# Stick-breaking attention: suffix sums in two float32r passes, mask by TensorE, both heads' exponentials together

## The reference

```python
z = jnp.einsum('bqhd,bkhd->bhqk', qb, kk).astype(jnp.float32) * scale
mask = (k_pos[None, :] < q_pos[:, None])[None, None]
log_beta = jax.nn.log_sigmoid(z)
log_one_minus = jnp.where(mask, jax.nn.log_sigmoid(-z), 0.0)
suffix = lax.cumsum(log_one_minus, axis=3, reverse=True) - log_one_minus
A = jnp.where(mask, jnp.exp(log_beta + suffix), 0.0)
outs.append(jnp.einsum('bhqk,bkhd->bqhd', A.astype(v.dtype), vv))
```

## Time and profile before

| | us |
|---|---|
| median of 3 runs | 4930.05 |
| lowest, highest | 4927.13, 4930.28 |
| the profiled execution | 4933.49 |
| its span, first to last instruction | 4931.4 |
| TensorE busy | 4438.4 (90%) |
| VectorE busy | 2837.3 (58%) |
| ScalarE busy | 1843.0 (37%) |
| mean granted TensorE clock | 0.958 |

### The profile page before, as it was taken

One profiled execution on the slowest core, in us unless ns is written; L12 is line 12 of the kernel. 1 busy time (PEld: TensorE's weight loads), 2 busy tenths in 40 slices (PEclk: granted clock), 3 DMA queues, 4 the chain that ended last, 5 costly groups with the idle time before them and its releaser, 6 DMA issues. The chain is left out here.

```text
span 4931.4 us, 59891 instructions
## 1 busy us (share of the span) xinstructions
PE 4438.4 (90%) x22171; PEld 3698.0 (75%) x22171; DVE 2837.3 (58%) x5051; ACT 1843.0 (37%) x2602; POOL 413.9 (8%) x308
## 2 busy tenths in 40 slices
PE   7988888878998466999999996999999999899998
PEld 5867775645874256999999995766878877677887
DVE  0777776683436897888888885334343333444332
ACT  1655644443321033333333333346232233643322
POOL 0000000000002601232222320000000000000000
PEclk9999999999999798999999998999999999999999
DMA  7111111102221036777777771211323322122232
GB/s 261 56 39 39 35 35 43 39 13 90 90 77 61 10 137 229 280 269 281 271 277 280 270 278 63 72 48 45 101 90 98 95 75 66 37 73 92 95 96 84
DMA packets 195952, 578.14 MB, mean 117 GB/s; under 512 B 17328, under 2 KB 66736, under 8 KB 194352
## 3 DMA queue, kind: packets, MB, share of 16 engines
q1 hardware_dynamic: 157888, 433.77, 25.9%
q0 software_dynamic: 36864, 134.23, 8.0%
q10 hardware_dynamic: 1008, 7.55, 0.4%
HBM read 548.22 MB, written 27.26 MB: 117 GB/s over the span
## 5 line engine op out<-in xcount | busy, mean ns | idle before, releaser
L402 DVE TENSOR_TENSOR tile_rest<-tile_raw,tile_up 128x1024 fp32r<-128x1024 f32 (+2 forms) x288 | 338.6, 1180 | 781.9 <-ACT tile_up L393 781.6
L410 PE MATMUL layer_psum<-hn_up,tile_up 128*128 128x512 f32 x1344 | 535.0, 398 | 21.2 <-DVE hn_rest L497 21.2
L411 PE MATMUL layer_psum<-hn_up,tile_rest 128*128 128x512 f32 x1344 | 527.3, 392 | 0.0
L412 PE MATMUL layer_psum<-hn_rest,tile_up 128*128 128x512 f32 x1344 | 527.0, 392 | 0.0
L393 ACT ACTIVATE tile_up<-tile_raw 128x1024 fp32r<-128x1024 f32 (+2 forms) x288 | 291.4, 1018 | 369.1 <-PE layer_psum L412 368.5
L2186 PE MATMUL ex_psum<-ex_t_up,ex_u_up 128*128 128x384 f32 x1024 | 344.5, 336 | 10.5 <-ACT ex_prod L2260 6.2
L2204 PE MATMUL ex_psum<-ex_prod_up,ex_v_up 128*128 128x384 f32 x1024 | 342.9, 335 | 3.9 <-DVE xT L2326 3.9
L2187 PE MATMUL ex_psum<-ex_t_up,ex_u_rest 128*128 128x384 f32 x1024 | 344.0, 336 | 0.0
L2188 PE MATMUL ex_psum<-ex_t_rest,ex_u_up 128*128 128x384 f32 x1024 | 343.9, 336 | 0.0
L2206 PE MATMUL ex_psum<-ex_prod_rest,ex_v_up 128*128 128x384 f32 x1024 | 342.6, 335 | 0.0
L2205 PE MATMUL ex_psum<-ex_prod_up,ex_v_rest 128*128 128x384 f32 x1024 | 342.6, 335 | 0.0
(11 more groups left out here) (440 smaller groups left out, 10140.1 us busy)
## 6 DMA issues: line engine op xcount, KB each, us to landing
ex_u<-in_peer_u SPq DMA_DIRECT2D x128, 512.0 KB, 6.8
tT<-in_peer_v SPq DMA_DIRECT2D x128, 512.0 KB, 7.4
tile_raw<-in_w_gu SPq DMA_DIRECT2D x88, 512.0 KB, 3.5
xT<-in_w_head SPq DMA_DIRECT2D x56, 512.0 KB, 3.5
mod_w<-in_w_ada SPq DMA_DIRECT2D x48, 512.0 KB, 4.8
mg_w_raw<-in_w_merge SPq DMA_DIRECT2D x48, 512.0 KB, 3.5
expert_table<-et_rows SPq DMA_DIRECT2D x6, 4096.0 KB, 13.3
ex_rows<-expert_table SPq DMA_DIRECT2D x64, 384.0 KB, 8.0
```

Of the source, the lines that this page charges most:

```text
L402: self.nc.vector.tensor_tensor(out=self.rest[:, n % self.SLOTS, 0:blocks, :], in0=self.raw[n % self.RAWS][:, 0:blocks, :], in1=self.up[:, ...
L410: self.nc.tensor.matmul(dst, w_up, up, start=first, stop=False)
L411: self.nc.tensor.matmul(dst, w_rest, up, start=False, stop=False)
L412: return self.nc.tensor.matmul(dst, w_up, rest, start=False, stop=last)
```

## The change

The scores' accumulation group gets one more float32r matmul per key block, which adds -2^30 at and below the diagonal of the block's first 128 columns. That takes the place of all eight multiplies by the mask. The scores go to SBUF in one VectorE copy of 1280 columns a head; ScalarE takes |z| straight from PSUM. The term that is summed becomes max(z, 0) + ln(1 + exp(-|z|)), in one VectorE instruction. ScalarE rounds it to float32r (`up`), VectorE takes the remainder (`low`), and the sums are twenty float32r matmuls a head with negative constants. The triangle includes the key itself, so z plus the sums is the power. ScalarE's order becomes |z|, exp, |z|, exp, ln, ln, and both projections stand ahead of both sums on TensorE. Three float32r constants are made by ScalarE at the start of layer 0's stage, and the first scores wait for them. `z` lies in the tables' memory, so layer 1's retention loads the tables again, and VectorE waits for that. Cut to its core:

```diff
-    AT = [0, 512, 896, 1152]
+    AT = [0, 512, 1024, 896]
@@ stage_retention
     def sync(sp):
         if first:
             w.load_to(sp, base + 2)
-            sp.dma_start(mem.tab[:], io["tables"]).then_inc(tables, 16)
+        else:
+            for powered in earlier.powered:
+                sp.wait_ge(powered, START + 12)
+        sp.dma_start(mem.tab[:], io["tables"]).then_inc(tables, 16)
         w.load_to(sp, sk + 10)
@@ vector
-            dve.wait_ge(tables, START + 16)
+        dve.wait_ge(tables, START + 16)
         for n in range(4):
             w.cut_rest(dve, q_of(0) + n + 4)
@@ stage_sticks, tensor
+            if layer == 0 and i == 0 and hh == 0:
+                pe.wait_ge(signs, START + 3)
             for c in ORDER:
-                nc.tensor.matmul(part(hh, c), k[rows, c * P:(c + 1) * P], q[rows, c * P:T],
-                                 start=True, stop=True).then_inc(scored[hh], 1)
+                nc.tensor.matmul(part(hh, c), k[rows, c * P:(c + 1) * P], q[rows, c * P:T], start=True, stop=False)
+                ins = nc.tensor.matmul(part(hh, c)[:, 0:P], mem.minus["far"][:], mem.minus["later"][:],
+                                       start=False, stop=True)
+            ins.then_inc(scored[hh], 1)
@@
-            pe.wait_ge(rested[hh], START + 3 * i + 3)
+            pe.wait_ge(low_ready[hh], START + i + 1)
...
+                    for piece in (up[hh], low[hh]):
+                        ins = nc.tensor.matmul(dst[:, (c2 - c) * P:T - c * P], sign, piece[:, AT[c2]:AT[c2] + n],
@@
             project(0, Q_AT[i + 1] if following else mx)
+            project(1, Q_AT[i + 1] + 1 if following else mx + 1)
             sums(i, 0)
-            project(1, Q_AT[i + 1] + 1 if following else mx + 1)
             sums(i, 1)
             output(i, 0)
@@ scalar
+        def exponentials(i, hh):
+            act.wait_ge(scored[hh], START + i + 1)
...
+            if i > 0 and hh == 0:
+                act.wait_ge(sb_cut, START + i)
+            nc.scalar.activation(beta[hh][:], every(hh), ACT.Abs).then_inc(soft[hh], 1)
+            act.wait_ge(soft[hh], START + i * 4 + 1)
+            nc.scalar.activation(beta[hh][:], beta[hh][:], ACT.Exp, scale=-1.0).then_inc(soft[hh], 1)
...
+        def halves(i, hh):
+            act.wait_ge(raised[hh], START + i + 1)
+            nc.scalar.activation(up[hh][:], beta[hh][:], ACT.Copy).then_inc(up_ready[hh], 1)
...
+        if layer == 0:
+            nc.scalar.activation(mem.minus["later"][:], mem.c("later"), ACT.Copy, scale=-1.0).then_inc(signs, 1)
+            nc.scalar.activation(mem.minus["ones"][:], mem.c("ones"), ACT.Copy, scale=-1.0).then_inc(signs, 1)
+            nc.scalar.activation(mem.minus["far"][:], mem.c("ident"), ACT.Copy, scale=-FAR).then_inc(signs, 1)
         for i in range(PAIRS):
+            exponentials(i, 0)
+            exponentials(i, 1)
             logs(i, 0)
             logs(i, 1)
...
+            between(i, 0)
+            halves(i, 0)
+            halves(i, 1)
+            tile(i, 0)
+            between(i, 1)
+            tile(i, 1)
+            weights(i, 0)
+            weights(i, 1)
@@ vector
         for i in range(PAIRS):
...
+            copies(i, 0)
+            copies(i, 1)
+            raises(i, 0)
+            raises(i, 1)
+            halves(i, 0)
+            halves(i, 1)
+            tile(i, 0)
+            powers(i, 0)
+            tile(i, 1)
+            powers(i, 1)
@@ constants
-           "later": (r[:, None] > r[None, :]) * 1.0,
-           "before": (r[:, None] < r[None, :]) * 1.0,
+           "later": (r[:, None] >= r[None, :]) * 1.0,
```

More of the change, by code:

```diff
@@ L42 @@
 CONSTS = [("ones", P), ("mean_d", P), ("mean_head", P), ("mean_ret", P), ("ident", P), ("swap", P),
-          ("later", P), ("before", P), ("iota", P), ("eps", 1), ("one", 1),
+          ("later", P), ("iota", P), ("eps", 1), ("one", 1),
           ("cos2", T), ("sin2", T)]
@@ L2403, with stage_retention @@
 Retention = namedtuple("Retention", "sync tensor scalar vector sk_out rstd_ready cut")
-Sticks = namedtuple("Sticks", "sync tensor scalar vector o_out sig_done cut")
+Sticks = namedtuple("Sticks", "sync tensor scalar vector o_out sig_done cut powered")
 Stage = namedtuple("Stage", "sync tensor scalar vector norm")
-def stage_retention(nc, io, mem, ph, local, layer, norm=None):
+def stage_retention(nc, io, mem, ph, local, layer, norm, earlier):
     F = 6
@@ L2745, in sums @@
                     n = T - c2 * P
-                    ins = nc.tensor.matmul(dst[:, (c2 - c) * P:T - c * P],
-                                           mem.c("later") if c2 == c else mem.c("ones"),
-                                           rest[hh][:, AT[c2]:AT[c2] + n], start=c2 == c, stop=c2 == TB - 1)
-                ins.then_inc(summed[hh], 1)
+                    sign = mem.minus["later"][:] if c2 == c else mem.minus["ones"][:]
+                    for piece in (up[hh], low[hh]):
+                        ins = nc.tensor.matmul(dst[:, (c2 - c) * P:T - c * P], sign, piece[:, AT[c2]:AT[c2] + n],
+                                               start=c2 == c and piece is up[hh],
+                                               stop=c2 == TB - 1 and piece is low[hh])
+                if c != 1:
+                    ins.then_inc(summed[hh], 1)
         def output(i, hh):
@@ L2856, in scalar @@
                 act.wait_ge(o_out[hh], START + i + 1)
-            nc.scalar.activation(mem.sb_up[:, i, :], o[:], ACT.Copy).then_inc(sb_up_ready, 1)
+            nc.scalar.activation(mem.sb_up[:, i, :], o, ACT.Copy).then_inc(sb_up_ready, 1)
         w.cut_up(act, mx + 6)
     def vector(dve):
-        def before(hh, data):
-            for c in range(TB):
-                ins = nc.vector.tensor_tensor(out=data[:, AT[c]:AT[c] + P], in0=data[:, AT[c]:AT[c] + P],
-                                              in1=mem.c("before"), op=ALU.mult)
-            return ins
@@ new lines, in raises, with halves @@
+        def raises(i, hh):
+            dve.wait_ge(soft[hh], START + i * 4 + 3)
+            dve.wait_ge(copied[hh], START + i + 1)
+            nc.vector.scalar_tensor_tensor(out=beta[hh][:], in0=z[hh], scalar=0.0, in1=beta[hh][:], op0=ALU.max,
+                                           op1=ALU.add).then_inc(raised[hh], 1)
+        def halves(i, hh):
+            dve.wait_ge(up_ready[hh], START + i + 1)
+            nc.vector.tensor_tensor(out=low[hh][:], in0=beta[hh][:], in1=up[hh][:].bitcast(F32),
+                                    op=ALU.subtract).then_inc(low_ready[hh], 1)
@@ L2879, in powers @@
         def powers(i, hh):
-            for c, made in zip(ORDER, MADE):
-                dve.wait_ge(summed[hh], START + i * TB + made)
-                cols = slice(AT[c], AT[c] + T - c * P)
-                nc.vector.tensor_tensor(out=beta[hh][:, cols], in0=beta[hh][:, cols], in1=part(hh, c),
+            for bank in range(3):
+                dve.wait_ge(summed[hh], START + i * 3 + bank + 1)
+                cols = slice(bank * 512, min(bank * 512 + 512, ALL))
+                nc.vector.tensor_tensor(out=z[hh][:, cols], in0=z[hh][:, cols], in1=every(hh)[:, cols],
@@ L2884, in powers, with tile @@
                                         op=ALU.add).then_inc(powered[hh], 1)
-        def weights(i, hh):
-            dve.wait_ge(a_raw[hh], START + i + 1)
-            before(hh, z[hh]).then_inc(a_ready[hh], 1)
+        def tile(i, hh):
+            w.cut_rest(dve, (Q_AT[i + 1] if i + 1 < PAIRS else mx) + 4 + hh)
         for i in range(PAIRS):
-            following = i + 1 < PAIRS
-            rests(i, 0)
-            rests(i, 1)
-            for hh in range(2):
-                powers(i, hh)
-                w.cut_rest(dve, (Q_AT[i + 1] if following else mx) + 4 + hh)
-                weights(i, hh)
+            copies(i, 0)
[8 more added lines that the diff above has]
+            powers(i, 1)
@@ L3172, in phase_layers @@
                     with ExitStack() as own:
-                        ret = stage_retention(nc, io, mem, ph, allocator(own), layer, norm)
+                        ret = stage_retention(nc, io, mem, ph, allocator(own), layer, norm, stick)
                     with ExitStack() as own:
@@ L3257, in build @@
                                   for part in ("up", "rest"))
+        mem.minus = {n: ctx.enter_context(nc.sbuf_tensor(f"minus_{n}", [P, P], F32R)) for n in ("later", "ones", "far")}
         phase_layers(nc, io, mem, out)
```

82 lines of the change are left out of this document (33 added, 49 removed).

## The result

The changed kernel takes 4938.91 us (median of 10 runs, 4931.8 to 4945.77), the kernel before 4928.85 beside it (10 runs, 4923.34 to 4934.37). The ratio is 1.0021, with an interval of 1.0013 to 1.0029: slower by 0.2%, at the edge of what can be told from no change. The forecast was 4900, in a range from 4874 to 4910. The profiled execution has a span of 4939.9 us against 4931.4, 8.5 more.

What follows compares the result with a forecast made beforehand. TensorE was taken as near its limit in the sticks stage, busy 263.1 of 287.64 us. Layers of 131.1 and 126.7 make 257.8, 29.8 less; 4933.5 - 29.8 = 4903.7, less 3.4 for the median: 4900.2, range 4874 to 4910.

Steps and rivals of the forecast that it cites:

- A pair lasts 28.5 us: Sticks stage: with no wait left before the sums, a head pair without value projection takes 28.5 us with hand-overs.
- the 2.0 that I allowed: Start of layer 0's stage: 2.0 us added for TensorE's low clock after 3.2 us idle.
- the 257.8 forecast: Sticks stage of both layers, eight head pairs: 257.8 us against 287.64 before, 29.8 us less.
- The mark that I set for it: Sticks stage in the changed profile: a clock below 0.9 would show the account of the pair to be wrong.
- Rival (C): Sticks stage: gaps between narrow float32r sums keep TensorE's clock low; 5070 at two thirds, 5150 over the whole; chance 0.03.
- Its decision point: Low-clock rival: each us at 0.5 costs 0.5, so it decides from 60 of the stage's 258 us on.
- 0.22: Price in us of each narrow 128-column float32r matmul, masks and sums alike, 24 a pair; the other end was 0.07.
- Rival (A): Masks and sums: narrow float32r matmuls are cheap, 0.12 or 0.07 us each; 4883 or 4878 us; chance 0.30.
- the waits of 2.6 and 2.8 us: TensorE before the first head's sums: waits of 2.58 and 2.79 us a pair vanish, with 0.7 to spare.
- rival (B): ScalarE leads: exp after the other head's |z| needs two more table loads a pair, 15 us given back; 4915; chance 0.07.
- The tables' transfer between the layers: Layer 1's table load takes 8.2 us but ends 11 us before VectorE's next cut, so its price is nothing.
- Rival (D): Sums stay behind ScalarE, waits only move and narrow matmuls at 0.22 gain nothing; 4925 to 4935; chance 0.04.

Runs made afterwards that it cites:

- e1: The changed kernel without TensorE's mask matmuls, so the output lacks the causal mask inside the diagonal blocks: 4880.33 us, ratio 0.9901.
- h1: The changed kernel with early constants and each mask replaced by a float32r matmul as wide as its block's scores (other values): 4951.55 us, one run.
- f2: The changed kernel with early constants and scores contracted over all 128 rows instead of a head's 64 (other values): 4880.14 us, one run.
- g4: The changed kernel with early constants and each float32r mask over the head's own 64 rows, half of it missing: 4885.52 us, one run.
- f3: The changed kernel with early constants and a head's masks in groups of two, after two blocks of scores: 4902.66 us, ratio 0.9941.
- g3: The kernel with VectorE's mask and the later sigmoid, with TensorE's order put back to projection, sums, projection, sums: 4957.61 us, ratio 1.0047.
- e4: The changed kernel with its three float32r constants made at the program's start: 4933.27 us, ratio 1.001.
- f4: The changed kernel with early constants and no masks on TensorE; VectorE adds -2^30 while copying the scores: 4890.21 us, ratio 0.9918.
- e3: The kernel before with early constants and eight mask matmuls a pair added behind its scores, its own multiplies kept: 4964.74 us, ratio 1.0071.
- f1: The changed kernel with early constants and the masks in plain float32 over 128 rows: 4920.79 us, ratio 0.9982.
- e2: The changed kernel without masks but with each head's scores issued twice: 4926.47 us, one run.
- g1: The kernel with VectorE's mask, and in the last pair the first gate's sigmoid moved behind the two roundings: 4890.54 us, ratio 0.9922.
- g2: The kernel with VectorE's mask and later sigmoid, with plain float32 sums in one pass, no rounding or remainder: 4898.34 us, ratio 0.9935.

## Why the prediction was wrong

**The step that failed is the clock.** "A pair lasts 28.5 us" silently takes 1.00 for TensorE's clock throughout. Stretch by stretch it was 0.80 to 0.91, 39 us in all, against the 2.0 that I allowed. 291.3 less these 37, with 2.5 for the start, is 256.8, against the 257.8 forecast. The mark that I set for it, a clock below 0.9 in the stage, was met in six pairs of eight.

**Rival (C) named the event, not its mechanism or its size.** It said that the clock would stay low because of gaps around narrow float32r sums. e1 has all of these sums at 1.00, and h1 has the loss with wide masks: it is the masks' place between the scores, not their narrowness and not the sums. Its decision point holds. It put the tie at 60 us of stretch at the lower level, and 39 us lost are 78 us at 0.5. It priced only two thirds and the whole of the stage, 5070 and 5150, a loss of 170 and 250 us; what came was 39, about 0.15 of the 258 us of work (4900 + 39 = 4939). Its tie counts measured time at the lower level and its two prices count work, so they can't be compared as they stand. At 0.03 its chance was too small. The rows of before gave no sign of it: the clock is below 1.00 in five of their eight pairs, and each fall stands behind a wait of 2.6 to 2.8 us before the sums, none among the scores. My argument against the rival looked at the projections, not at the new sequence, for which no row stood.

**The price of a mask was half of the true one.** 0.22 was asked to hold for eight masks and sixteen narrow sums alike. A mask costs 0.42 to 0.49 (the two changes of rows at its sides, by f2, g4 and f3), so eight were priced some 2 us a pair too low; a narrow sum costs 0.11, so sixteen were priced 1.8 us too high. The two errors cancel, and this is why 28.3 us at full clock looks like a confirmed 28.5. A price that is bounded by two ends and used for two kinds of neighbours is two prices. Rival (A) had the sums right with 0.12, and its 26.0 a pair is what f2 and g4 measure (26.10, 25.72): it is the time with the changes of rows gone, which (A) did not price.

**Right:** the waits of 2.6 and 2.8 us went, and nothing took their place, since both projections cover ScalarE's chain (g3 shows their worth). The 0.85 us stayed at the end of the second pair. The first scores wait 2.5 us for the constants (forecast 2.4), and with the clock behind that they cost 5.6 us where 4.4 were forecast (e4). ScalarE loads its table for ln and exp eight times in the four pairs. The kernel before did so seventeen times, the twelve of the earlier trace rows and these five for the exponential of the power:

```profile
L2827 ACT ACT_TABLE_LOAD x5 | 6.4, 1283 | 0.1
```

So rival (B) did not come. The tables' transfer between the layers holds up nobody; VectorE's next tile cut waits for ScalarE. The rows of the changed kernel for these three, the start of the stage in TensorE's timeline, the loads in the groups of layer 0's stage, and VectorE's timeline between the layers:

```profile
3286.73 2.04 PE L2748 MATMUL layer_psum<-sk_q,sk_k 64*128 64x512 f32 x2 [3.26 <-ACT minus_far L2862]
```
```profile
L2834 ACT ACT_TABLE_LOAD x4 | 5.1, 1283 | 0.1
L2843 ACT ACT_TABLE_LOAD x4 | 5.1, 1283 | 0.1
```
```profile
4013.90 2.59 DVE L402 TENSOR_TENSOR tile_rest<-tile_raw,tile_up 128x1024 fp32r<-128x1024 f32 x2 [4.58 <-ACT tile_up L393]
```

Rival (D), that the waits only move, ended nearest to the measured time and was wrong in all its steps. The change does what it says; without its masks on TensorE it is worth 40 us (f4, 4890.21 against 4930.71 beside it).

**Still open** is what sets the fall off. Counted over the eight pairs of each profiled execution, away from the wait for the constants, it comes in all of them with single float32r matmuls over 128 rows among the 64-row float32 scores (the changed kernel, e3, e4, h1). It comes in one pair with the longer float32 ones (f1), in one with grouped ones (f3), in two with masks over 64 rows (g4), in one of seven with doubled scores and no masks (e2). It comes in none with scores over 128 rows (f2) and in none with 64-row scores and no mask (e1, f4, g1, g2; f4's 0.94 stands behind its wait of 2.15 us). So neither the change of rows nor the kind is needed for a fall, and neither alone makes it come every time: f1 has as many changes of rows, and g4 and f2 have the same kinds beside each other. Removing either makes it rare here. The runs give how often it happens under which conditions, each from one profile, and not what sets it off.

**The best version** is the one that masks on VectorE, f4 or g1: 0.992 of the kernel before and 0.990 of the changed one (4890.2 to 4938.9). Grouping the masks (f3) keeps them on TensorE at 0.994.

## What to carry to other kernels

Moving a small step onto TensorE cost more than its columns here (0.42 to 0.49 us a mask against 0.11), because it interrupts a run of matmuls with another number of rows: keep its rows equal to its neighbours', or put several together, and compare the run of matmuls before and after it, not only the new one. Read the granted clock of the stretch before believing a sum of TensorE durations, and keep a case of its own for it with a price for a part of the stretch (39 of 291 us were lost here), also where TensorE has no wait left. Where one unknown price is used for instructions with different neighbours, give each its own.

## What the runs showed of the hardware that I had not expected

- The granted clock of TensorE can go from the 2.4 GHz level (1.00) to the 1.2 GHz level (0.50) within a few us while TensorE is busy for 100% of the time. The Trainium skill (TensorE: Matmul & The Clock Gate, "Why this matters for your kernels") advises against long idle gaps between bursts of matmuls; here no gap over 0.85 us stood ahead of seven of the eight pairs, and they lost 30.6 of the 39 us. So the advice was followed there and the clock was lost all the same; the measurement decides.
- A change between 64-row and 128-row matmuls costs 0.14 to 0.20 us each way at full clock (0.42 to 0.49, 0.30 and 0.105 to 0.15 us for a mask with two, one and no change).
- A float32r matmul with 128 moving columns and its own weight block costs 0.11 us in a run of its kind, 0.06 from the first to the second of a pair.
- The same instructions in the same order ran at 1.00 in one layer and at 0.77 in the other (e2), and, in f1, at 0.81 and 1.00.
